# A ring of 14 weight tiles in place of 15 in the expert stage of a hybrid decoder block

## The reference: what is computed

```python
logits = (xt @ w_router + b_router).astype(jnp.float32)
top_val, top_idx = lax.top_k(logits, TOP_K)          # 4 of 32
gates = jax.nn.softmax(top_val, axis=-1)
def expert_block(args):
    xblk, e = args
    gu = xblk @ w1[e] + b1[e]                        # 1024 -> 2048
    g, up = gu[:, :D_FF], gu[:, D_FF:]
    g = jnp.minimum(g, SWIGLU_LIMIT)
    up = jnp.clip(up, -SWIGLU_LIMIT, SWIGLU_LIMIT)
    act = (up + 1.0) * g * jax.nn.sigmoid(SWIGLU_ALPHA * g)
    return act @ w2[e] + b2[e]                       # 1024 -> 1024
```

## Time and profile before

| what | value |
|---|---|
| time, median of 3 runs | 1368.07 us |
| the profiled execution: its time | 1372.02 us |
| the profiled execution: its span | 1370.2 us |
| TensorE busy (matmul) | 1173.8 us, 86% |
| bytes moved | 467.03 MB, mean 341 GB/s |
| expert tiles: loads of 1 MB, median from issue to landing | 256 "in" 26.2 us, 128 "out" 26.5 us |

### The profile page before, as it was taken

The page is one execution under the profiler, slowest core; times in us unless marked ns, Lnnn a source line. Parts: engine busy times, 40 slices in busy tenths (PEclk is TensorE's granted clock), DMA queues, the critical chain, the costliest instruction groups (busy, mean ns, idle before and its releaser), DMA issues.

```text
span 1370.2 us, 16028 instructions
## 1 busy us (share of the span) xinstructions
PE 1173.8 (86%) x6509; PEld 598.7 (44%) x6509; DVE 376.8 (28%) x683; ACT 143.0 (10%) x303; POOL 148.8 (11%) x199
## 2 busy tenths in 40 slices
PE   3667679999699979997999979999889999789874
PEld 2455247785545423333444424544334443334322
DVE  5699887622511011111111110201101111001101
ACT  2000002221201100010101000101001010100001
POOL 4666553000200000000000000000000000000000
PEclk9889779999697999998999998999999999999986
DMA  9833446574280999999999999999999999999995
GB/s 321 297 113 122 142 173 224 199 296 192 110 330 23 368 421 420 421 422 420 421 406 421 421 421 421 409 421 421 421 421 412 421 421 421 420 414 417 420 421 245
DMA packets 88880, 467.03 MB, mean 341 GB/s; under 512 B 12451, under 2 KB 13560, under 8 KB 39652
## 3 DMA queue, kind: packets, MB, share of 16 engines
q1 hardware_dynamic: 81648, 459.72, 82.7%
q0 software_dynamic: 1760, 5.11, 1.2%
q10 hardware_dynamic: 5396, 1.14, 0.4%
HBM read 464.88 MB, written 3.16 MB: 342 GB/s over the span
## 4 chain that ended last, share of the span: by engine, by line
SPq 37%; PE 33%; DVE 11%; DMA 10%; issue 4%; POOL 3%; ACT 2%; DVEq 0%; ACTq 0%; POOLq 0%
SPq L534 36%; DMA ring_w<-in_w_exp_out 10%; PE psum L726 6%; PE psum L1072 5%; PE psum L992 4%; DVE work L1474 3%; PE psum L1001 3%; PE psum L996 3%; PE psum L739 2%; PE psum L1028 2%; PE psum L934 1%; PE psum L1096 1%; DVE work L1559 1%; PE psum L715 1%; DMA cst<-in_const 1%
## 5 line engine op out<-in xcount | busy, mean ns | idle before, releaser
L996 PE MATMUL psum<-ring_w,xe 128*64 128x512 f32 x960 | 215.6, 597 | 13.5 <-DMA ring_w<-in_w_exp_in 13.5
L1751 DVE TENSOR_SCALAR row_a<-psum 128x512 f32<-128x512 f32 (+1 forms) x37 | 22.4, 605 | 665.5 <-PE psum L1015 465.4
L1001 PE MATMUL psum<-ring_w,xe 128*32 128x256 f32 x1536 | 108.0, 428 | 40.3 <-DMA ring_w<-in_w_exp_in 39.1
L996 PEld LDWEIGHTS psum<-ring_w,xe 128*64 128x64 f32 x960 | 64.8, 137 | 156.1 <-issue 114.0
L1074 PE MATMUL psum<-ring_w,aT 128*64 128x512 f32 x480 | 117.5, 612 | 6.5 <-DMA ring_w<-in_w_exp_out 6.0
L992 PE MATMUL psum<-ring_w,xe 128*128 128x512 f32 x256 | 114.2, 598 | 4.1 <-DMA ring_w<-in_w_exp_in 4.1
L726 PE MATMUL psum<-hT,ring 128*128 128x256 f32 x448 | 107.7, 400 | 9.0 <-DMA ring<-in_w_in 9.0
L586 POOL TENSOR_SCALAR small<-small 128x1 f32<-128x1 f32 x8 | 1.5, 188 | 1018.6 <-ACT row_g L1380 992.6
L726 PEld LDWEIGHTS psum<-hT,ring 128*128 128x128 f32 x448 | 88.2, 200 | 27.0 <-issue 14.7
L1001 PEld LDWEIGHTS psum<-ring_w,xe 128*32 128x32 f32 x1536 | 48.2, 119 | 97.1 <-DMA ring_w<-in_w_exp_in 60.8
L1328 ACT ACTIVATE row_b<-row_a 128x512 f32<-128x512 f32 (+1 forms) x37 | 20.7, 559 | 570.0 <-DVE row_a L1751 570.0
(11 more groups left out here) (289 smaller groups left out, 1052.7 us busy)
## 6 DMA issues: line engine op xcount, KB each, us to landing
ring_w<-in_w_exp_in SPq DMA_DIRECT2D x256, 1024.0 KB, 26.2
ring_w<-in_w_exp_out SPq DMA_DIRECT2D x128, 1024.0 KB, 26.5
ring<-in_w_ada SPq DMA_DIRECT2D x12, 2048.0 KB, 15.6
ring<-in_w_in SPq DMA_DIRECT2D x8, 2048.0 KB, 10.9
ring<-in_w_out SPq DMA_DIRECT2D x2, 2048.0 KB, 10.9
ring<-in_w_glu SPq DMA_DIRECT2D x1, 2048.0 KB, 8.7
ring<-in_w_att_out SPq DMA_DIRECT2D x1, 2048.0 KB, 7.8
ring<-in_w_ssm_out SPq DMA_DIRECT2D x1, 2048.0 KB, 12.4
```

Source lines behind the costliest of these rows:

```text
L996: mm = pe.matmul(bank[b][64 * n:64 * n + 64, :], rows[:, k, :], w[:, FF * b + 512 * n:FF * b + 512 * n + 512], start=k == 0, stop=False, t ...
L1001: mm = pe.matmul(bank[0][32 * n:32 * n + 32, 256 * b:256 * b + 256], rows[:, k, :], w[:, FF * b + 256 * n:FF * b + 256 * n + 256], start=k ...
```

## The change

The ring of the experts' weights has 14 slots instead of 15. The first 14 slots keep their places. The memory of the fifteenth stays set aside under a name that nothing uses (`gap0`), so that every tensor behind it keeps its address.

```diff
-SLOTS = 15
+SLOTS = 14
 SLOT_W = 2048
-SLOT_AT = [8, 9, 10, 11, 2, 3, 4, 5, 6, 7, 0, 1, 12, 13, 14]
+SLOT_AT = [8, 9, 10, 11, 2, 3, 4, 5, 6, 7, 0, 1, 12, 13]
@@
         ring_w = sb("ring_w", [P, SLOTS, SLOT_W])
+        sb("gap0", [P, SLOT_W])
         xe = sb("xe", [P, 2, KD, XE_W])
```

## The result

| | before | after |
|---|---|---|
| time, median | 1368.08 us (5 runs, 1367.25 to 1368.87) | 1375.01 us (5 runs, 1374.41 to 1378.49) |
| ratio to before | | 1.0055, 95% interval 1.0040 to 1.0069 |
| the profiled execution: time, span | 1372.02, 1370.2 us | 1374.58, 1372.8 us |

The account below looks back on a forecast made before the run. From about 460 us the DMA stream of weights was taken as the bound; start 2.5, three stretches 5.1 and the last 2.1 gave +9.7 us on 1368.07, so 1377.8 us; own range 1375.5 to 1380.5, 8-in-10 range 1374.0 to 1381.5.

Parts of the forecast that it names:

- the two kinds of places: Where SP waits on the ring: the start, and the four big places p = 9, 15, 21, 27.
- The start: After the pause near 413 to 442 us the weight stream restarts one load short: +2.49 us.
- The big places: At p = 9, 15, 21, 27 the held tiles delay loads: +1.7 us for each of three stretches, +2.1 the last.
- the fresh load: First load issued 3.68 us after a big place's last "out" tile lands; forecast to land after 4.8 us, not 6.2.
- the rival of a faster stream: Whole stream from 460 us on: fewer loads under way shorten each; at 2%, -8.2 us, 1359.9; chance 0.03.
- a cost above the bound: At the big places idle TensorE drops to 1.2 GHz: up to 14.8 us more, 1392.6; chance 0.07.
- 5.1 + 2.1 = 7.2: Big places: 5.1 us for three stretches between them, 2.1 us for the last stretch to the last landing.
- S' = 1.5: Time per stretch after a big place in which single engines fall behind, from instruction fetches: 1.5 us with 14 slots.
- second dips: A further rate dip behind the fresh load at each big place, seen at 691 to 692.5 us: about 0.4 us.
- The upper bound: At each big place most engines lack slack, so one load less costs the whole 2.49 us; sum at most 12.5 us.
- only the slowest engine counts: At each big place only the last engine's lag of 1.1 us costs: +6.9 us in all, 1375.0; chance 0.16.

Follow-up runs that it names:

- the start alone: 15 slots, but loads 14 to 59 wait in addition for the tile 14 loads back, against the kernel before: 1371.52 us, ratio 1.0012.
- the big places alone: 15 slots, but at p = 9, 15, 21, 27 loads also wait for the tile 14 loads back, against the kernel before: 1374.99 us, ratio 1.0034.

## Why the prediction was right, and where it was off

The change was forecast at +9.7 us, 1377.8, in a range of 1374.0 to 1381.5; it measured +6.9, 1375.01. The direction, the two kinds of places and the cause were right. The number itself is helped by a wide range: 1375.01 lies just below the forecast's own range (1375.5 to 1380.5) and inside the stated one because that was drawn down to take in the rival at 1375.0. By the stages the change is 8.3 us, which would be 1376.4.

*The start.* Forecast +2.49, measured +2.47 in the kernel after and +2.44 with the start alone. TensorE's third "out" tile of p = 1 is now

```profile
469.07 1.07 PE L1065 MATMUL psum<-ring_w,aT 128*32 128x256 f32 x16 [1.40 <-DMA ring_w<-in_w_exp_out]
```

The forecast had said that this one wait, 0.34 us in the earlier trace rows, would be about 2.5 us longer; it is 1.1 longer. The rest stands ahead of it, in waits of 0.25 and 0.84 us that the kernel before did not have. From the end of the pause these matmuls start after 30.59 us, where it was 28.15: 2.4 us later in all.

*The big places, the mechanism.* Right: the 3.68 us to the issue are unchanged, the fresh load lands after 4.8 to 5.2 us, the H runs keep 421 GB/s (which leaves nothing for the rival of a faster stream), TensorE's clock stays at 1.00 at the big places (which leaves nothing for a cost above the bound), and keeping the tiles for a shorter time takes the cost away.

*The big places, the size.* The four stages grew by 5.9 us, where 5.1 + 2.1 = 7.2 was forecast: the stretches are 182.1, 181.3 and 182.3 us, each against 182.2, and the last is 128.3 against 128.7. The step that was off is the term S' = 1.5, "no less than one fetch of 1.1 and hardly two". "All engines are starved at the big place and start level again" is borne out by the landings. The rest of the sum, with the measured landing of the fresh load (5.2, 4.8, 5.2, 4.8 us, forecast 4.8) and the measured delay of the load behind it (0.3, 0.4, 0.6, 0.6 us, forecast 0.4) put in, leaves 1.1, 0.6, 1.0 and 0.9 us for S'. The fresh landings and second dips, a little longer than forecast, hid part of this miss. S' is a remainder here, and no run shows why it stays under one fetch.

The upper bound was too strong in "Most engines therefore have no slack at all". The windows of 20 us show what an engine loses on average: 1.9 us at the first place and 1.0 to 1.4 at the others, not 2.49. The share of 0.83 that the sentence rested on came from the first place. In the first 3 us behind the issue the kernel before had 328 GB/s there, but 347, 369 and 371 at the other three.

*A forecast of the profile that failed.* I expected 300 to 320 GB/s in the 13 us behind the issue. It was 359, 372, 362 and 366 at the four places, since the engines had begun to run empty before the issue. A window must begin where the queue does, not where the issue is.

*The rest.* 8.3 us in the stages against 6.9 in the medians is within the interval (up to 9.4), and the repeat of the kernel before has a span of 1364.7 where the first had 1370.2. The rival "only the slowest engine counts" named 1375.0 and met the median, but by luck, for its stages are wrong: it has 1.1 us at each place, 4.4 in all, against 5.9 in the kernel after and 6.0 with the big places alone. What it leaves out is the load behind the fresh one, which comes late too, by 0.3 to 0.6 us.

*What the forecast did not look for.* It took the pause in the earlier trace rows as given. Its length is a matter of the order in which the slots are taken. That order was worth 15 us, more than the change.

## What to carry to other kernels

In this kernel a slot taken from the ring cost nothing where the DMA stream was saturated (421 GB/s with 15, 14 and 13 slots). It cost where the consumer holds many tiles at once, and where the stream restarts after a pause. Look for such places by the first short issue after a long wait, and price them by the bytes that the window around them lacks. Before paying for more slots, compare the order in which tiles come free with the order in which they are overwritten: taking the slots in the consumer's order made this kernel 1.2% faster, and a slot less then cost 0.5 us by the medians and 0.6 by the stages.

## What the runs showed of the hardware that was not expected

The stages between big places repeated within 0.3 us in the two profiles of the kernel before. With 14 slots at the big places they differed by up to 0.8 us between two profiles, while their sum kept to 0.1 us. The first part varied by 4 us and the tail by 1.8 us. In the tail the same 16 matmuls took between 1.11 and 1.98 us, by the clock that was granted just then.

A 1 MB load that finds the DMA engines all but idle landed after 4.8 to 5.2 us, with some ten others ahead of it after 26 to 29 us. The stretches between big places last about 1.6 us longer than 72 loads at 2.485 us (178.9 us). I put this down to instruction fetches that hold up single engines (8 packets in such a stretch). The trace agrees: a packet of that queue takes 1.1 us, and behind a packet, at the next load or two to land, the 16 parts of a load together come about 1.5 us late, as if one engine alone were held up (the packets at 708.3, 734.7 and 755.1 us in the kernel before, with the loads that land at 711.2, 738.6 and 758.5). No experiment changed the number of these fetches, so that they make up the whole 1.6 us stays an argument. Why the middle stretch grew by 1.0 us only is open; with the big places alone it grew by 1.7.
